# Moving the tiles of a two-layer hybrid decoder to 2048-byte starts in SBUF, and narrowing the row pitch of its activations

## What is computed

```python
for l in range(DEPTH):
    x = layer_norm(ALPHA * x + 0.5 * swiglu(x, ffn1_w_in[l], ffn1_w_out[l]), ...)
    mix = hybrid_mixer(x, mix_w_in[l], ..., mix_w_out[l])
    x = layer_norm(ALPHA * x + mix, ln2_g[l], ln2_b[l])
    x = layer_norm(ALPHA * x + memory_cross_attn(x, mem, ...), ln3_g[l], ln3_b[l])
    x = layer_norm(ALPHA * x + 0.5 * swiglu(x, ffn2_w_in[l], ffn2_w_out[l]), ...)
```

## Time and profile before

| | |
|---|---|
| three runs | 2221.10, 2223.02, 2223.25 us |
| the profiled execution | 2221.10 us, span 2219.3 us |
| PE busy | 2167.4 us, 98% of the span |
| VectorE, ScalarE, GpSimd busy | 1088.6, 833.2, 1000.5 us |
| granted TensorE clock, mean | 0.998 |

### The profile page before, as it was taken

How to read it: one execution, slowest core, us unless ns; L and a number is a source line. 1 busy time by engine, 2 the same in 40 slices (tenths; PEclk the granted TensorE clock), 3 DMA queues, 4 the chain that set the end, 5 groups by cost and what they waited for, 6 DMA issues and landing times. The chain is left out here.

```text
span 2219.3 us, 26951 instructions
## 1 busy us (share of the span) xinstructions
PE 2167.4 (98%) x11052; PEld 1813.0 (82%) x11052; DVE 1088.6 (49%) x1194; ACT 833.2 (38%) x1168; POOL 1000.5 (45%) x416
## 2 busy tenths in 40 slices
PE   7999999999999999999999999999999999999997
PEld 6888889788778888888888888897786888888886
DVE  2433335887746633323443333359877475333234
ACT  3322224935344522222363222257365345222223
POOL 5444444445543544444364444454365335444442
PEclk9999999999999999999999999999999999999999
DMA  4333322333322233332233333323243222333321
GB/s 170 95 99 100 115 92 71 86 103 103 107 87 67 77 98 101 95 116 96 74 96 95 100 102 107 101 58 95 87 123 106 86 67 79 99 98 95 114 93 50
DMA packets 96043, 210.91 MB, mean 95 GB/s; under 512 B 39344, under 2 KB 52016, under 8 KB 95664
## 3 DMA queue, kind: packets, MB, share of 16 engines
q1 hardware_dynamic: 93536, 205.55, 30.2%
q10 hardware_dynamic: 2384, 3.64, 0.5%
HBM read 207.06 MB, written 2.10 MB: 94 GB/s over the span
## 5 line engine op out<-in xcount | busy, mean ns | idle before, releaser
L534 POOL TENSOR_TENSOR w_lo<-raw,w_hi 128x1024 fp32r<-128x1024 f32 (+2 forms) x358 | 931.7, 2604 | 1191.4 <-ACT w_hi L1226 1191.3
L1226 ACT ACTIVATE w_hi<-raw 128x1024 fp32r<-128x1024 f32 (+2 forms) x358 | 401.4, 1121 | 1210.3 <-PE psum L622 1136.3
L616 PE MATMUL psum<-acts_hi,w_hi 128*128 128x512 f32 x1744 | 684.1, 392 | 3.0 <-ACT tmp L1594 3.0
L619 PE MATMUL psum<-acts_lo,w_hi 128*128 128x512 f32 x1744 | 678.8, 389 | 0.0
L622 PE MATMUL psum<-acts_hi,w_lo 128*128 128x512 f32 x1744 | 430.7, 389 | 0.0
L616 PEld LDWEIGHTS psum<-acts_hi,w_hi 128*128 128x128 f32 x1744 | 327.4, 188 | 75.6 <-issue 3.9
L619 PEld LDWEIGHTS psum<-acts_lo,w_hi 128*128 128x128 f32 x1744 | 327.5, 188 | 69.5 <-issue 2.4
L622 PEld LDWEIGHTS psum<-acts_hi,w_lo 128*128 128x128 f32 x1744 | 327.4, 188 | 67.9
L1832 DVE TENSOR_TENSOR work<-work,psum 128x512 f32<-128x512 f32 x85 | 58.4, 687 | 563.7 <-PE psum L622 538.8
L616 PE MATMUL psum<-h_hi,w_hi 128*128 128x512 f32 x616 | 239.6, 389 | 0.0
L619 PE MATMUL psum<-h_lo,w_hi 128*128 128x512 f32 x616 | 239.6, 389 | 0.0
(11 more groups left out here) (305 smaller groups left out, 2459.1 us busy)
## 6 DMA issues: line engine op xcount, KB each, us to landing
raw<-w_in SPq DMA_DIRECT2D x176, 512.0 KB, 3.6
raw<-w_out SPq DMA_DIRECT2D x64, 704.0 KB, 4.0
raw<-w_kv SPq DMA_DIRECT2D x32, 512.0 KB, 3.6
raw<-w_mix SPq DMA_DIRECT2D x26, 512.0 KB, 3.6
raw<-w_q SPq DMA_DIRECT2D x16, 512.0 KB, 3.6
raw<-w_o SPq DMA_DIRECT2D x16, 512.0 KB, 3.6
raw<-w_v SPq DMA_DIRECT2D x4, 768.0 KB, 4.3
raw<-w_mix SPq DMA_DIRECT2D x24, 128.0 KB, 3.3
```

The costliest lines, as they stand in the source:

```text
L534: nc.gpsimd.tensor_tensor(w_lo[:, n % SPLIT, 0:width], raw[:, n % RAW, 0:width], w_hi[:, n % SPLIT, 0:width].bitcast(F32), ALU.subtract).t ...
L616: nc.tensor.matmul(o, hi, b_hi, start=start and k == 0, stop=False)
L619: nc.tensor.matmul(o, hi, b_lo, start=False, stop=False)
L1226: A(w_hi[:, n % SPLIT, 0:width], raw[:, n % RAW, 0:width], ACT.Copy).then_inc(w_hi_made, 1)
```

## The change

Both fillers grow by 64 elements (256 bytes), and PITCH falls from 576 to 544 elements, 2304 to 2176 bytes. No instruction, wait, size of an operand or order is touched. Worked out from the declared sizes: `x` starts at byte 18,432, `acts_hi` at 34,816, `acts_lo` at 52,224, `raw` at 69,632, `w_hi` at 94,208, `w_lo` at 106,496, `work` at 118,784, `consts` at 126,976, the region at 137,216. All are multiples of 2048 except `acts_lo`, which is 1024 beyond one. The rows of `acts_hi`, `acts_lo`, `z2_hi` and `z2_lo` step by 2176 bytes, so the odd rows start 128 beyond a multiple of 256, where all eight started at a multiple of 256 before.

```diff
-ROW, PITCH = SEQ + 2, SEQ + 64
+ROW, PITCH = SEQ + 2, SEQ + 32
...
-        sb("to_256", [P, 16])
+        sb("to_2048", [P, 80])
         x = sb("x", [P, KT, SEQ])
         acts_hi = sb("acts_hi", [P, KT, PITCH], F32R)
         acts_lo = sb("acts_lo", [P, KT, PITCH], F32R)
...
-        sb("to_256_again", [P, 56])
+        sb("to_2048_again", [P, 120])
```

## The result

The changed kernel takes 2244.18 us (median of four runs, 2244.04 to 2244.62) against 2223.11 us of the kernel before beside it (four runs, 2221.10 to 2223.25). The ratio is 1.0097, with a 95% interval of 1.0080 to 1.0114: slower by 21.1 us. The forecast of no change was wrong.

The account below looks back on a forecast made before the run. TensorE's matmul count times the distance between starts was taken as the bound. All terms were 0, giving 2221.10 us for the profiled execution; the median, 1.9 us above it, was forecast at 2223.0 us, range 2219 to 2227.

Parts of the forecast that it names:

- What bounds the kernel: TensorE, busy 98% of the span: time is the number of matmuls times the distance between starts, almost nothing else.
- Multiples of 256: Even rows of acts, weights, hidden tiles and region tiles: new starts on such multiples change matmul distance by 0 ns.
- Odd rows, "I take 0": TensorE's full-row matmuls reading acts rows 128 beyond a multiple of 256: 0 us taken, between bounds 0 and 34.8.
- The rival of the odd rows: Moving rows at odd multiples of 128 lengthen 2616 TensorE matmuls by 6.7 ns: 17.5 us, 2240.5 us; chance 0.07.
- The rival of the gap: Added 13.3 ns per float32r matmul come from misplaced operands and go: 82 us faster, 2141 us; chance 0.02.
- Fills, DMA and waits: Writes filling acts 0 (to 1.0 us), transfers 0, TensorE's waits unchanged within 2.5 us either way.

Follow-up runs that it names:

- align_only: Kernel before with the first filler widened by 64 elements, PITCH 576 and the second filler kept: 2221.92 us, ratio 1.0001.
- weights_by_128: Kernel before with raw, w_hi, w_lo, work, consts, mats and var moved by 128 bytes, activations and region left in place: 2267.53 us.
- all_by_128: Kernel before with the first filler widened by 32 elements, so every tile from x on moves by 128 bytes, distances between tiles unchanged: 2221.55 us.
- acts_lo_by_128: Kernel before with 128 bytes between acts_hi and acts_lo and 128 behind acts_lo, so only acts_lo moves: 2235.53 us.

## Why the prediction was wrong

**What bounds the kernel** held: TensorE's matmul count times their distance, with waits that didn't move.

**Multiples of 256** held. Starts on 512 and 2048 give 0 for the activations and the weights (`align_only`) and for the hidden tiles (7.48 us in the changed kernel). The argument, that moving rows and weights already stand at every multiple of 256 from each other, used the quantity that counts; but it said nothing of other distances.

**Odd rows, "I take 0"** is the step that failed. The bounds, 0 and 34.8 us, held the measured 23.3 us of the profile; the value was taken from the wrong end. The reason given was that three kinds of row show no dependence on 128, 36 or 4 bytes. Two of them, VectorE's taps and ScalarE's copy, are other engines. The third, L955, is plain float32 with 96 columns. None of them is a float32r matmul streaming a full row beside a weight load, which is what the change touched. Plain float32 could hardly have shown it: `weights_by_128` moves `consts` by 128 bytes against `x` and `tmp`, and by the starts in the two traces the matmuls that read them stay where they were, 429 ns apart with 512 columns (L759, whose stationary operand is one column repeated; median of 4) and 109 ns in the transposes of 128 columns (L1115; median of 64). In place of the 0 the runs showed 107 ns for each activation tile, 8.9 ns a row if it is put on the 12 odd ones. The right reading of an empty place in the trace would have been wide odds.

**The rival of the odd rows** (0.07, 17.5 us, 2240.5 us) came closest: 2244.18 us. Its side, its engine and its lines were right, its size 3.6 us short. The size was in part luck: its 6.7 ns was half of a bound and no reading, and the changed kernel has 8.9. Its mechanism was only half right: it is not the row's start but its distance from the weights, as `all_by_128` shows. Put on the chain, it foresaw 5.52 us and unchanged hidden tiles; measured were 5.547 and 7.480.

**The rival of the gap** fell: the 13.3 ns that each float32r matmul adds at the best distance stayed at all distances tried, in the full rows. Only the 256-column matmuls lost some of it, at 64 and 32 bytes off.

**Fills, DMA and waits** were 0 as said, to some tenths: L549 1286 for 1292 ns, L1318 632 ns, the first wait 12.4 for 12.0 us.

Of the loads the Trainium skill says in "SBUF — State Buffer", "Who interferes with whom", that TensorE has two independent read ports, one for the moving operand and one for LDWEIGHTS, and that it never waits on anyone. The runs here don't fit with that: moving `w_hi` and `w_lo` by 32 to 128 bytes, with nothing else of the work changed, costs 5.7 to 6.7 ns in each full-row matmul. They don't show that one read waits for the other.

**What stays open.** The inner mechanism was not shown, only that the distance modulo 256 between moving row and weights decides whether there is a loss; that it is the two reads at once is inferred from the timeline. How large the loss is doesn't follow from the distances alone: the two levels at 128 bytes and the mixed pitches show that. With PITCH 544 twelve rows of 24 are off and cost 107 ns, 8.9 ns each, where eight single ones cost 6.7 each; by starts, the rows that agree are longer there too. In that layout the first 16 rows go two by two (high and low row k agree, high and low row k + 1 don't), which `acts_lo_by_128` doesn't have. Whether that pairing is why was not tried; PITCH 528 has it too, with more rows off and a smaller extra. No version faster than the kernel before came out of this; its distances are all at the free value already.

## What to carry to other kernels

Where float32r matmuls with full 512-column rows bound a kernel, keep the start of each moving row and of each stationary tile equal modulo 256 bytes (here 0 was the only free distance among 0, 32, 64 and 128), and therefore the pitch of both a multiple of 256; where they both stand made no difference in the three places tried (`all_by_128`, `align_only`, the kernel before). When a change touches a form of instruction that the trace has not shown under the new condition, other engines and shorter or wider types are weak evidence for it, and a cheap test is to move everything together and then one side alone.

## What the runs showed of the hardware

Float32r matmuls of 512 columns start 226.7 ns apart at full clock when moving row and weights agree modulo 256 bytes, and, where every row is off, 233.3 ns at 32 and 64 bytes, and 232.4 or 233.3 ns at 128, by the stretch of the kernel. Float32r matmuls of 256 columns start 120 ns apart when they agree and 114 when they are 64 off. Plain float32 matmuls stay at 429 ns (L759, 512 columns) and 109 ns (L1115, 128 columns) when their operands move by 128 bytes against each other. VectorE's taps (755 ns), GpSimd's L549 (1286 ns) and ScalarE's L1318 (632 ns) show nothing of the kind in the changed kernel.
